# A two-layer S5/attention/MoE backbone: the scan's lag rows computed in four column groups, a chunk's state reordered, four transfers a round instead of eight

## The reference, cut to what matters

```python
def scan_direction(seq, d):
    lam_bar = jnp.exp(lam * dt)
    b_bar = ((lam_bar - 1.0) / lam)[..., None] * lax.complex(b_re[d], b_im[d])
    bu = jnp.einsum('blgh,gph->blgp', ug.astype(jnp.complex64), b_bar)
    _, states = lax.associative_scan(_recurrence_combine, (a, bu), axis=1)
def readout(states, d):
    y = jnp.einsum('blgp,ghp->blgh', states, cm).real
y_lat = readout(st_f[:, n_ctx:], 0) + readout(st_b[:, :n_lat], 1) + dsk * u_lat
```

## Time and profile before

| | us |
|---|---|
| median of 3 runs | 1863.85 (1862.78 to 1872.2) |
| the profiled execution | 1866.43 |
| its span in the trace | 1864.7 |
| PE busy | 1688.1 (91%) |
| DVE busy | 706.2 (38%) |
| ACT busy | 418.5 (22%) |
| POOL busy | 303.9 (16%) |
| layer 0: input matrices and scan / readout rounds | about 62 to 188 / 188 to 312 |
| layer 1: the same | about 1133 to 1253 / 1253 to 1358 |

### The profile page before, as it was taken

The page is one execution under the profiler, slowest core; times in us unless marked ns, Lnnn a source line. Parts: engine busy times, 40 slices in busy tenths (PEclk is TensorE's granted clock), DMA queues, the critical chain, the costliest instruction groups (busy, mean ns, idle before and its releaser), DMA issues.

```text
span 1864.7 us, 28853 instructions
## 1 busy us (share of the span) xinstructions
PE 1688.1 (91%) x11470; PEld 1024.0 (55%) x11470; DVE 706.2 (38%) x1564; ACT 418.5 (22%) x866; POOL 303.9 (16%) x263
## 2 busy tenths in 40 slices
PE   5999998989999999899988988998889999996697
PEld 2467555554444443456545556676557888453354
DVE  4578764650110112311101158696763111421123
ACT  4011112551000001322222250111144001331133
POOL 0004342770000000200000020045464000000000
PEclk9999998899999999999999989999889999997899
DMA  9311469219222153499999633125661346899981
GB/s 392 125 46 30 143 228 344 47 46 348 103 96 84 68 225 130 174 369 356 386 392 393 229 115 113 46 74 199 219 121 55 150 176 241 344 401 411 411 350 59
DMA packets 108139, 384.07 MB, mean 206 GB/s; under 512 B 42016, under 2 KB 61472, under 8 KB 68864
## 3 DMA queue, kind: packets, MB, share of 16 engines
q1 hardware_dynamic: 61040, 329.14, 45.6%
q10 hardware_dynamic: 42720, 22.72, 5.4%
q0 software_dynamic: 4272, 30.67, 4.8%
HBM read 363.09 MB, written 31.98 MB: 212 GB/s over the span
## 4 chain that ended last, share of the span: by engine, by line
PE 63%; DVE 12%; DMA 8%; SPq 6%; POOL 4%; issue 3%; ACT 3%; ACTq 1%; POOLq 0%; DVEq 0%
PE tile_ps L599 55%; SPq L535 6%; PE turn_ps L599 4%; DMA arena<-sorted_in 3%; POOL arena L2007 2%; DMA vn<-in_wpack 2%; PE out_ps L599 1%; DMA ring<-in_wpack 1%; PE turn_ps L920 1%; DVE arena L1870 1%; DMA x<-in_xT 1%; DMA arena<-in_rpb 1%; DVE smx L1852 1%; DVE arena L1515 1%; DVE arena L1562 1%
## 5 line engine op out<-in xcount | busy, mean ns | idle before, releaser
L599 PE MATMUL tile_ps<-h,ring 128*128 128x512 f32 (+1 forms) x1312 | 472.0, 514 | 6.7 <-ACT h L1130 5.0
L599 PEld LDWEIGHTS tile_ps<-h,ring 128*128 128x128 f32 x1312 | 250.0, 192 | 211.1 <-issue 195.5
L599 PE MATMUL tile_ps<-arena 128*32 128x256 f32 (+5 forms) x3152 | 270.1, 351 | 25.6 <-POOL arena L1997 5.8
L599 PE MATMUL tile_ps<-arena,ring 128*128 128x512 f32 (+1 forms) x704 | 235.3, 486 | 2.7 <-issue 2.7
L599 PEld LDWEIGHTS tile_ps<-arena 128*32 128x32 f32 (+4 forms) x3152 | 180.7, 140 | 84.0 <-issue 41.8
L599 PEld LDWEIGHTS tile_ps<-arena,ring 128*128 128x128 f32 x704 | 133.6, 190 | 96.6 <-issue 87.6
L2007 POOL TENSOR_SCALAR arena<-arena,smx 128x512 f32<-128x512 f32 (+1 forms) x96 | 129.1, 1362 | 74.0 <-DVE smx L1858 73.6
L599 PE MATMUL tile_ps<-ring,arena 128*32 128x256 f32 (+2 forms) x1008 | 95.9, 428 | 20.9 <-DMA ring<-in_wpack 14.4
L1344 ACT ACTIVATE arena<-tile_ps 128x512 f32<-128x512 f32 (+1 forms) x56 | 27.5, 491 | 347.3 <-PE tile_ps L599 347.3
L1891 DVE TENSOR_TENSOR arena<-tile_ps,arena 128x512 f32<-128x512 f32 (+1 forms) x32 | 17.9, 558 | 212.2 <-PE tile_ps L599 212.2
L599 PEld LDWEIGHTS tile_ps<-ring,arena 128*32 128x32 f32 (+1 forms) x1008 | 49.8, 125 | 57.2 <-issue 41.1
(11 more groups left out here) (316 smaller groups left out, 2272.0 us busy)
## 6 DMA issues: line engine op xcount, KB each, us to landing
ring<-in_wpack SPq DMA_DIRECT2D x176, 1024.0 KB, 7.6
arena<-in_wpack SPq DMA_DIRECT2D x64, 1024.0 KB, 16.0
h<-in_wpack SPq DMA_DIRECT2D x15, 1024.0 KB, 24.8
qa<-in_wpack SPq DMA_DIRECT2D x12, 1024.0 KB, 9.2
qn<-in_wpack SPq DMA_DIRECT2D x12, 1024.0 KB, 12.4
kn<-in_wpack SPq DMA_DIRECT2D x12, 1024.0 KB, 14.5
vn<-in_wpack SPq DMA_DIRECT2D x12, 1024.0 KB, 16.6
sorted_out<-arena ACTq DMA_DIRECT2D x44, 128.0 KB, 7.7
```

The source lines that it names most:

```text
L599: return nc.tensor.matmul(out, lhsT, rhs, start=start, stop=stop)
```

## The change

z(q) now writes group g of the round to partitions 32g to 32g+15 of the two banks, in columns 0 to 127, where all four groups stood side by side on partitions 0 to 15. Its loop has the real and imaginary part outside and the group inside. So `zs`, `dsk` and the copies that make them have 128 partitions and a quarter of the elements in each. The rows of `tm` (and with them the partitions of `ug`, the columns of `wm`) are ordered by channel first and reversed step second. With that order the rows of one group are eight windows per channel, each 16 elements further, which one transfer can describe: four transfers of 128 rows of 512 bytes a round (64 KB each), two on ACT's queue and two on SP's, where eight of 64 rows of 512 bytes (32 KB each) were.

```diff
-ON_SP = 4
+ON_SP = 2
-        dsk, a0 = cut(a0, [NGRP, GRP], parts=GRP)
+        dsk, a0 = cut(a0, [NQ, GRP])
-        wm, a1 = cut(a1, [2, GQ, STEP, GRP])
+        wm, a1 = cut(a1, [2, GQ, GRP, STEP])
-        zs, _ = cut(SSM["bre"].start, [GQ, (2 * STEP - 1) * GRP], parts=GRP)
+        zs, _ = cut(SSM["bre"].start, [(2 * STEP - 1) * GRP])
+        def lag_rows(g):
+            v = zs[32 * g:32 * g + GRP, 0:P]
+            (step, n), (one, m) = v.ap
+            return bass.AP(tensor=v.tensor, offset=v.offset, ap=[[step, n], [GRP, STEP], [one, m]])
...
-                    for j in range(STEP - ON_SP, STEP):
-                        a = (STEP - 1 - j) * GRP
-                        sp.dma_start(tm[j * GRP:(j + 1) * GRP, q % 2], zs[:, :, a:a + P]).then_inc(tm_in, 16)
+                    for g in range(GQ - ON_SP, GQ):
+                        sp.dma_start(tm[:, q % 2, g], lag_rows(g)).then_inc(tm_in, 16)
...
-                        for g in range(GQ):
-                            at_q = (q % 2) * GQ + g
-                            for r in range(2):
+                        for r in range(2):
+                            for g in range(GQ):
+                                at_q = (q % 2) * GQ + g
                                 for n, (d, lags) in enumerate(((lower, slice(0, STEP)), (upper, slice(2, NPOS)))):
-                                    ins = mm(bank((l, "z", q, n))[0:GRP, g * P:(g + 1) * P], bb[d, r, q * GQ + g, :],
+                                    ins = mm(bank((l, "z", q, n))[32 * g:32 * g + GRP, 0:P], bb[d, r, q * GQ + g, :],
...
-                act.dma_start(ug, u_dram.rearrange("j t (a g) c -> (j t a) g c", g=NGRP)).then_inc(ug_in, 16)
+                act.dma_start(ug, u_dram.rearrange("j t (a g) c -> (t a) j (g c)", g=NGRP)).then_inc(ug_in, 16)
...
-                        copy(job, zs[:, :, (STEP - 1) * GRP:], bank(job)[0:GRP].rearrange("p (g n) -> p g n", g=GQ))
+                        copy(job, zs[:, (STEP - 1) * GRP:], bank(job)[:, 0:P])
...
-                        for j in range(STEP - ON_SP):
-                            a = (STEP - 1 - j) * GRP
-                            act.dma_start(tm[j * GRP:(j + 1) * GRP, q % 2], zs[:, :, a:a + P]).then_inc(tm_in, 16)
+                        for g in range(GQ - ON_SP):
+                            act.dma_start(tm[:, q % 2, g], lag_rows(g)).then_inc(tm_in, 16)
...
-                CP(zs[:, :, 0:(STEP - 1) * GRP], back[:, :, 0:(STEP - 1) * GRP]).then_inc(zd_done, 1)
+                CP(zs[:, 0:(STEP - 1) * GRP], back[:, 0:(STEP - 1) * GRP]).then_inc(zd_done, 1)
...
-                TT(zs[:, :, mid], zs[:, :, mid], dsk[:, q * GQ:(q + 1) * GQ, :], ALU.add).then_inc(zd_done, 1)
+                TT(zs[:, mid], zs[:, mid], dsk[:, q, :], ALU.add).then_inc(zd_done, 1)
...
-                    free(job, CP(up[:, m].rearrange("p (j c) -> p j c", j=STEP),
+                    free(job, CP(up[:, m].rearrange("p (j c) -> p j c", j=STEP)[:, ::-1],
                                  bank(job).rearrange("p (c j) -> p j c", j=STEP)))
...
-                    pv = [spread(pww[:, r, :, gs].rearrange("p j g -> p g j"), 3, GRP) for r in range(2)]
-                    bv = [spread(bb[:, r, gs, :], 2, STEP) for r in range(2)]
+                    pv = [spread(pww[:, r, :, gs].rearrange("p j g -> p g j"), 2, GRP) for r in range(2)]
+                    bv = [spread(bb[:, r, gs, :], 3, STEP) for r in range(2)]
```

More of the change, by code:

```diff
@@ L1519, in readout_rows @@
                 if q:
[L1520 removed]
+                    dve.wait_ge(tm_in, 16 * GQ * (l * NQ + q))
                 job = (l, "z", q, 1)
[L1522 removed]
+                back = bank(job)[:, 0:P]
                 mid = slice((STEP - 1) * GRP, STEP * GRP)
                 wait_full(dve, job)
[L1525 removed]
+                CP(zs[:, 0:(STEP - 1) * GRP], back[:, 0:(STEP - 1) * GRP]).then_inc(zd_done, 1)
                 wait_taken(dve, (l, "z", q, 0))
[L1527 removed]
+                free(job, TT(zs[:, mid], zs[:, mid], back[:, mid], ALU.add))
                 wait_taken(dve, job)
[L1529 removed]
+                TT(zs[:, mid], zs[:, mid], dsk[:, q, :], ALU.add).then_inc(zd_done, 1)
             def scan_blocks(l):
```

21 lines of the change are left out of this document (9 added, 12 removed).

## The result

The changed kernel is slower: 1894.18 us (median of 4 runs, 1892.4 to 1896.4) against 1865.69 for the kernel before beside it, a ratio of 1.0135 with a 95% interval of 1.0103 to 1.0166. Timed again later it came to 1.0140 (1.0111 to 1.0169). The prediction had 1863 and a range up to 1873: it misses by 31 us, and the time lies outside the range.

The account below looks back on a forecast made before the run. It took DVE's chain to bound most of layer 0's rounds and POOL's loop layer 1's; layer 0 -4.0, layer 1 -2.6 and wm +6.3 gave -0.3 on 1863.85, so 1863.6, stated as 1863, range 1851 to 1873.

Parts of the forecast that it names:

- Part 1: PE's z in each round: column groups run side by side, z falls from 1.85 to 0.64 us, saving 1.2.
- Rival 4: z on PE stays at 1.85 us; readout, round 5 and wm effects remain: about 1867, chance 0.08.
- the 1.0 us: z's time on PE if each matmul has the skill page's overhead of about 60 cycles, plus drain.
- Part 2: Scan rounds: earlier y starts POOL at s + 3.6, holding DVE's products; each DVE-bound round 0.5 us longer.
- rival 2: POOL does not get between L1564 and L1565: 1857, or 1851 without wm's cost; chance 0.24.
- PE idles 1.7 us more in it: In each DVE-bound round lengthened by 0.5 us, PE was said to idle 1.7 us more.
- Part 3: ACT and SP issue two transfers each instead of four; layer 0's round 5 saves 1.9 us.
- Part 4: wm phase: four of six DVE products read strided, +0.35 us each; +6.3 us together on the path.
- The upper bound of 0.47 us: Largest extra time per strided wm product, from ACT's strided-read rate less 1.1 ns, over 512 elements.
- the term 6.3: wm's strided reads on the path: 2.8 us in layer 0 and 3.5 in layer 1, together +6.3 us.
- Rival 1: The strided read in wm costs nothing: -6.6 us, 1857; chance 0.17.
- Rival 3: POOL starts ahead of L1564, holding three DVE products, 1.33 us more in eight rounds: +10.6, 1874; chance 0.12.

Follow-up runs that it names:

- b_poolwait: The changed kernel plus one wait: POOL's products of a round wait until DVE has finished the previous round's readout copies; 1.0062, 1879.37 us.
- a_contig: The changed kernel with the powers that wm's products read stored contiguously again, so only the strided read is undone; 1.0116, 1887.25 us.
- c_both: The changed kernel with contiguous powers and POOL's wait for DVE's readout copies together; 1.0049, 1875.76 us.
- c_again: The kernel c_both unchanged, timed again beside j_all; 1.0001, 1865.15 us.
- g2_fill: The changed kernel plus one unread matmul ahead of qk_ms and one ahead of the projection, rounds 1 to 4 only; 1.0066, 1878.56 us.
- l_contig_fill: The changed kernel with contiguous powers and the added matmuls of g2_fill, POOL still starting early; 1.0048, 1874.2 us.
- d_oldz: The changed kernel with z back in one column group; strided wm, row order and four transfers stay; 1.0066, 1880.23 us.
- e_oldz_contig: The changed kernel with z in one column group and contiguous powers, leaving row order, gather and four transfers; 1.0017, 1866.54 us.
- m_strided_fill: j_all with the strided powers back and two added matmuls ahead of wm of round 3 in layer 0; 0.9966, 1861.4 us.
- j_all: c_both plus unread matmuls at all of PE's longer waits seen in the trace; 0.9934, 1856.21 us.
- h_zfill: c_both plus two unread matmuls ahead of z in layer 1's rounds 2, 5, 6 and 7; 0.9995, 1861.62 us.
- g_fill: The changed kernel plus two unread matmuls ahead of qk_ms and two ahead of the projection, rounds 1 to 7, both layers; 1.0147, 1891.35 us.
- i_gather: c_both with the gather of u split, each quarter fetched once it is in the scratch tensor; 1.0116, 1886.54 us.

## Why the prediction was wrong, step by step

- **Part 1, z in column groups: right.** 0.37 us for the 32 weight loads and 0.67 to y's first, where 0.64 had been said. Rival 4 (z no faster) and the 1.0 us by the Trainium skill's page TensorEngine Tiling (Array Packing), section Performance Considerations, are both excluded by that row: 32 weight loads in 0.37 us are 12 ns apart, under the 25 that its 60 cycles make.
- **Part 2, the early y: the mechanism right to a tenth or two, the consequence missed.** POOL at s + 3.60, L1569 held, L1533 held: each of these was said. L1818 ends 0.3 later (s + 7.27 against 6.97) and a round takes 17.12 us at full clock against 16.8, so 0.3 more where 0.5 had been said. With L1569 at 1.40 us rival 2 (POOL does not get in between) is out. Two things failed. First, the sum put the cost at the end of DVE's chain alone and overlooked that L1531, which stands behind the held L1569, frees the bank that qk_ms waits for: of PE's 1.7 us of extra idling, which the text names, 1.23 come in one piece, soon after the short z and y. (In the round shown, PE's waits go from 0.56 to 1.23 us; the rest of the 1.7 is taken up by the slower matmul behind them.) Second, and this is the step that failed: "PE idles 1.7 us more in it" was priced at the wall-clock time alone, with nothing for the clock. What the runs show in its place: the half-clock time of the rounds goes from 38 to 92 us. Taking POOL's early start away gains 14 us beside the changed kernel (b_poolwait) and 17 without the stride (a_contig against the mean of c_both and c_again; 12 against c_both alone); filling the waits gains 14 (g2_fill) and 13 (l_contig_fill against a_contig). Since g2_fill leaves DVE's chain as it is and only gives PE more to do, its 14 us are the clock's. Whether they are the same microseconds as b_poolwait's is not shown: no kernel has POOL's wait and g2_fill's matmuls together. Nor is it settled what lets the clock fall. A longer wait is one thing ahead of it, but the short z goes along with it in every kernel: c_both has 102 us of half clock without the collision, and d_oldz, with the long z, has 44.
- **Part 3, transfers: right, and a little more.** ACT's two issues in round 5 take 1.47 us instead of 3.86 (about 2 had been said), and PE's wait for `mrow` there falls from 3.4 to 0.77 us.
- **Part 4, `wm`: the lines right, the path in layer 0 too short.** 1.04 and 0.69 us a line, as said. (The upper bound of 0.47 us is 0.37 by the text's own numbers, 1.8 - 1.1 ns over 512; the value taken is under both.) What the stride costs in all, with and without it in otherwise equal kernels, is 9 us (d_oldz, e_oldz_contig), 7 (b_poolwait, the mean of c_both and c_again; 2 against c_both alone, which ran beside it), 4 (the changed kernel, a_contig), 3 (g2_fill, l_contig_fill) and 6 (m_strided_fill, j_all); the mean is 5 to 6, the term 6.3. Each pair alone is uncertain by as much, so they bear the term out and do not prove it. The profiles are sharper on one part. Layer 0's `wm` phase had 2.8 us in the sum. From 75 to 185 us the lag against before grows by 6.0 to 6.4 us in the four kernels of these pairs that have the stride and nothing in PE's wait, and shrinks by 0.5 to 2.4 in their partners: 7 to 8.5 us for the stride, with 10 to 15 us more at half clock. With that wait filled it is 4.4 (m_strided_fill, j_all). It is the same omission as in part 2. Rival 1 (the stride is free) is out by the lines themselves. The Trainium skill's page SBUF — State Buffer, section Door 1: The DMA port swizzle, whose note says that an access to a new 16-byte line pays a penalty, is borne out for an engine's read by 1.04 against 0.69 us.
- **Not in the sum: the gather of u.** The diff moves it and the front says so, but no term priced it. It lands 2.3 us later; in layer 1 PE's wait grows by 1.2 in the changed kernel and by 2.0 in c_both. With the row order and the transfers it comes to 3 us (e_oldz_contig, 0 to 7).
- **Rivals.** Rival 3, the slower one, had POOL ahead of L1564 and 1874; POOL did not get there. The time on the slower side came by a mechanism that the text named in half a sentence at its end (a clock that falls in the longer idle) and gave neither a size nor a chance. The earlier trace rows held its price: 5 us at half clock cost 2.5. With 38 us of half clock in the rounds of before, and PE's waits in each of layer 0's DVE-bound rounds going from 0.56 us to more than 2 by the text's own numbers, a rival "the half-clock time doubles, +15 to +20 us" could have been worked out from those rows and should have had a chance of 0.2 or more, with the range up to 1885.

As a sum at measured sizes: 6 for the stride, 3 for gather, row order and transfers, and the rest, 26 - 9 = 17 us (by the mean ratio of 1.0138 less those two), for the early y, of which 13 to 14 come back when PE's waits in the rounds 1 to 4 are filled, and more when the later ones are filled too (j_all, which also has POOL's wait). Each of these numbers is uncertain by 3 to 7 us. What the rounds 5 to 8 of layer 1 lose, and why there, no run takes apart.

The Trainium skill has the rule, on the page TensorE: Matmul & The Clock Gate, section Part 1: The HAM clock gate (the "warmup" mystery): "the default state is throttled, and activity releases the throttle". The trace agrees in the mean of a stage: 0.86 without and 1.00 with the added matmuls in the same window of the rounds.

## What to carry to other kernels

A wait of PE can have two prices: its own length and what the matmuls behind it cost if the clock is at half. Before a change that shortens PE's work at a place where another engine sets the round, count by stage how much time PE already spends at half clock, and give "this grows with the idling" a size and a chance of its own. If the waits can't be removed, cheap matmuls into an idle bank may pay for themselves, but only if they are shorter than the wait, by their measured length and not by an estimate.

## What the hardware showed that I had not expected

- PE's granted clock fell behind waits of 1.1 to 2.3 us, and in some executions behind one of 0.22 us, in rounds where PE's work is short; behind the same wait in the same code it stayed up in another execution (c_both and h_zfill above), and in g_fill it was down once with no wait of PE marked in the 23 us before. The kernel before itself ran from 1858 to 1878 us over some 90 runs, on the whole the slower ones at a lower mean clock (0.967 at 1859 us, 0.956 at 1877.5).
- The time at half clock in the phase of `wm` went from 3 to 17 us with one wait of 2.14 us, and was 3 again where added matmuls filled it (m_strided_fill).
- A transfer of 1024 KB in rows of 8 KB lands after 7.2 us instead of 4.9 when the rows are read in another order than they lie in; a quarter of it, to 32 partitions, is not quick either: in i_gather PE's matmuls on `ug` start 5.7 us after the last quarter's issue (1162.28 to 1167.98).
- The weight loads of 32 small matmul records over four column groups and two row halves start 12 ns apart.
